# Modulation parts: transposes and a sum on VectorE in place of folding matmuls, in a two-layer trunk on one core

## What is computed

```
silu_c = jax.nn.silu(c)
mod = silu_c @ p["w_mod"][l] + p["b_mod"][l]
sh1, sc1, gt1, sh2, sc2, gt2 = jnp.split(mod[:, None, :], 6, axis=-1)
h = rmsnorm(x, p["norm1_g"][l]) * (1.0 + sc1) + sh1
...
x = x + gt1 * mix
h = rmsnorm(x, p["norm2_g"][l]) * (1.0 + sc2) + sh2
x = x + gt2 * hier_moe(h, p, l)
```

## Time and profile before

| | us |
|---|---|
| median of 3 runs | 1727.54 (1727.22 to 1728.41) |
| profiled execution, its own time | 1724.3 |
| its span, first to last instruction | 1722.7 |
| TensorE busy (matmuls) | 1675.0 |
| VectorE busy | 526.5 |
| ScalarE busy | 258.2 |
| GpSimd busy | 46.2 |

### The profile page before, as it was taken

One profiled execution on the slowest core, in us unless ns is written; L12 is line 12 of the kernel. 1 busy time (PEld: TensorE's weight loads), 2 busy tenths in 40 slices (PEclk: granted clock), 3 DMA queues, 4 the chain that ended last, 5 costly groups with the idle time before them and its releaser, 6 DMA issues. The chain is left out here.

```text
span 1722.7 us, 20395 instructions
## 1 busy us (share of the span) xinstructions
PE 1675.0 (97%) x8346; PEld 968.2 (56%) x8346; DVE 526.5 (31%) x1265; ACT 258.2 (15%) x502; POOL 46.2 (3%) x93
## 2 busy tenths in 40 slices
PE   6999999999999899999999999999999998999997
PEld 3677764445577554444447777554547765444443
DVE  1220210124611354333442212102263126233346
ACT  3110001101210231111131100010112013211111
POOL 0000000000100000000000000000010010000000
PEclk8999999999999989999999999999999999999999
DMA  9533556467943649999983336443887432899993
GB/s 400 235 138 125 217 201 256 179 245 296 406 188 135 244 148 388 421 421 421 423 345 132 127 120 256 184 147 148 327 347 301 147 134 112 329 422 421 421 421 162
DMA packets 47021, 451.69 MB, mean 262 GB/s; under 512 B 5632, under 2 KB 5888, under 8 KB 7504
## 3 DMA queue, kind: packets, MB, share of 16 engines
q1 hardware_dynamic: 43200, 409.65, 59.6%
q10 hardware_dynamic: 3456, 37.75, 5.2%
q0 software_dynamic: 272, 2.97, 0.4%
HBM read 411.16 MB, written 39.19 MB: 261 GB/s over the span
## 5 line engine op out<-in xcount | busy, mean ns | idle before, releaser
L657 PE MATMUL ps<-ring,work 128*64 128x512 f32 x1536 | 337.9, 595 | 2.9 <-ACT work L1055 2.6
L657 PE MATMUL ps<-ring,hT 128*32 128x128 f32 (+1 forms) x1920 | 319.9, 383 | 2.1 <-DMA ring<-stream 2.0
L657 PE MATMUL ps<-hT,ring 128*128 128x288 f32 x1280 | 314.4, 407 | 1.9 <-DVE work L1608 1.9
L657 PEld LDWEIGHTS ps<-hT,ring 128*128 128x128 f32 x1280 | 242.2, 190 | 71.6 <-issue 6.1
L657 PE MATMUL ps<-work,ring 128*128 128x288 f32 x1024 | 249.6, 406 | 4.1 <-issue 2.3
L657 PEld LDWEIGHTS ps<-ring,hT 128*32 128x32 f32 (+1 forms) x1920 | 154.8, 137 | 168.1 <-issue 163.0
L1055 ACT ACTIVATE work<-ps 128x512 f32<-128x512 f32 (+5 forms) x244 | 109.5, 467 | 837.4 <-PE ps L657 836.5
L657 PEld LDWEIGHTS ps<-ring,work 128*64 128x64 f32 x1536 | 111.7, 137 | 211.3 <-issue 211.0
L657 PEld LDWEIGHTS ps<-work,ring 128*128 128x128 f32 x1024 | 194.2, 190 | 58.7 <-issue 5.4
L657 PE MATMUL ps<-work 128*128 128x288 f32 (+6 forms) x800 | 189.5, 399 | 6.3 <-DVE hT L1751 2.6
L657 PEld LDWEIGHTS ps<-work 128*128 128x128 f32 (+2 forms) x800 | 125.1, 187 | 69.4 <-issue 36.4
(11 more groups left out here) (177 smaller groups left out, 846.8 us busy)
## 6 DMA issues: line engine op xcount, KB each, us to landing
ring<-stream SPq DMA_DIRECT2D x96, 2048.0 KB, 8.6
ring<-stream SPq DMA_DIRECT2D x192, 1024.0 KB, 10.2
state_sample_out<-ring ACTq DMA_DIRECT2D x16, 2048.0 KB, 10.0
state_out<-prm ACTq DMA_DIRECT2D x8, 512.0 KB, 11.4
prm<-params SPq DMA_DIRECT2D x1, 2608.5 KB, 25.8
prm<-params POOLq DMA_DIRECT2D x1, 2608.5 KB, 15.8
cst<-consts SPq DMA_DIRECT2D x1, 1649.0 KB, 19.2
xT<-x_in SPq DMA_DIRECT2D x1, 1152.0 KB, 5.4
```

Source lines behind the costliest of these rows:

```text
L657: return nc.tensor.matmul(out, lhsT, rhs, start=start, stop=stop, **k)
```

## The change

Each folding product with modfold becomes a plain transpose against the identity: fold_pending writes four 128x128 transposes into a tile modt of its own, one for each mod step. The four partial sums then lie side by side along the free axis (in each chunk of 128 columns, four blocks of 32, of which 9 columns are used). VectorE sums them with one tensor_reduce per mod step over a strided view, waits, and adds the bias (take_mod in place of take_mods). It does so at the next "mod" step of its own list or at the "fold" step, so VectorE now waits on TensorE 24 times for these tiles, where it was 6. The table of banks changes: modt tiles mostly take turns over banks 0 to 6; the last of "next" and of "gate" lie in bank 7, those of "last" in banks 3 and 4. Nothing moves among the loads, the products or ScalarE's copies.

```diff
+turn, waiting = 0, None
+def use_fold(b=None):
+    global turn, waiting
+    if waiting is not None:
+        use((*waiting, "modt"), turn % 7 if b is None else b)
+        turn += b is None
+    waiting = None
...
-        for _g in (g for g, group in GROUPS_OF_MODS.items() if _s == ("mod", group[0])):
-            use((_g, "modt"), YBANK)
         for _t in tiles_of(_s, _l):
             use((_l, _s, _t), turn % 7)
             turn += 1
+        if _s[0] == "mod" or _s[0] == "fold" and waiting is not None and FOLD_OF[waiting[1][1]][0:2] == (_l, _s[1]):
+            use_fold(YBANK if _s in (("fold", "next"), ("fold", "gate")) else None)
+        if _s[0] == "mod":
+            waiting = (_l, _s)
...
-            if LAST_MODS[_l]:
-                use(((_l, "last"), "modt"), 3)
+            for _n, _s in enumerate(LAST_MODS[_l]):
+                use((_l, _s, "modt"), 3 + _n)
...
                 l, step = pending.pop()
-                gl, name, n = FOLD_OF[step[1]]
-                key = ((gl, name), "modt")
-                wait_reads(pe, [(l, step, "modp")], free=key if n == 0 else None)
+                key = (l, step, "modt")
+                out = wait_free(pe, key, [(l, step, "modp")])
                 buf = modp[:, MOD_TURN[step[1]] % 2, :]
                 for c in range(4):
-                    at = (4 * n + c) * ROWS
-                    last = mm(ps[bank(key)][:, at:at + ROWS], buf[:, c * P:c * P + P], C("modfold"), True, True)
-                if n == len(GROUPS_OF_MODS[gl, name]) - 1:
-                    made(last, key)
+                    last = transposed(out[:, c * P:c * P + P], buf[:, c * P:c * P + P], C("ident"))
+                made(last, key)
...
-            def take_mods(group):
-
-                l, first = GROUPS_OF_MODS[group][0]
-                n = 4 * len(GROUPS_OF_MODS[group])
-                bias = (R("bmod") if l == 0 else bias_next)[:, 4 * first:4 * first + n].rearrange("p (f o) -> p f o", o=1).broadcast_to([P, n, ROWS])
-                out = wait_made(dve, (group, "modt"))
-                taken(dve.tensor_tensor(mod_of(l)[:, 4 * first:4 * first + n, :], cut(out[:, 0:n * ROWS], n, ROWS), bias, ALU.add), (group, "modt"))
+            waiting = []
+
+            def take_mod(group=None):
+
+                if not waiting or group is not None and FOLD_OF[waiting[0][1][1]][0:2] != group:
+                    return
+                key = (*waiting.pop(), "modt")
+                l, i = key[1][1]
+                bias = (R("bmod") if l == 0 else bias_next)[:, 4 * i:4 * i + 4].rearrange("p (f o) -> p f o", o=1).broadcast_to([P, 4, ROWS])
+                dst = mod_of(l)[:, 4 * i:4 * i + 4, :]
+                parts = wait_made(dve, key)[:, :].rearrange("p (c j r) -> p c r j", c=4, j=4)[:, :, 0:ROWS, :]
+                taken(dve.tensor_reduce(dst, parts, op=ALU.add, axis=AX.X), key)
+                settle()
+                dve.tensor_tensor(dst, dst, bias, ALU.add)
                 settle()
```

More of the change, by code:

```diff
@@ L133, in use @@
     used[b] += 1
-turn = 0
+turn, waiting = 0, None
[5 more added lines that the diff above has]
+    waiting = None
 for _l in range(DEPTH):
@@ L1544, in _ @@
                     kind, i = step
-                    if kind == "fold":
-                        if step == ("fold", "start"):
+                    if kind == "mod":
+                        if l == 0 and step == ("mod", (0, 0)):
                             dve.wait_ge(head_loaded, 48)
-                        take_mods((l, i))
+                        take_mod()
+                        waiting.append((l, step))
+                    elif kind == "fold":
+                        take_mod((l, i))
                     elif kind == "scale":
@@ L1565, in _ @@
                             if i == 1:
-                                take_mods((l - 1, "last"))
+                                for last in LAST_MODS[l - 1]:
+                                    waiting.append((l - 1, last))
+                                    take_mod()
                     elif kind == "affine":
```

## The result

| kernel | median us (range) | executions |
|---|---|---|
| before | 1727.97 (1727.22 to 1729.64) | 4 |
| after | 1711.07 (1708.35 to 1712.45) | 4 |

The profiled execution of after took 1712.45 us by its own time, 11.85 less than that of before (1724.3). So of the 16.9 us one pair of profiles shows about 70%, and the rest has to be found in the executions beside it.

The account below looks back on a forecast made before the run. TensorE, busy for 1675.0 of 1722.7 us, was taken to bound the kernel. Savings of 3.5 + 0.5 + 1.07 + 2.0 + 2.18 = 9.2 us off a 1727.5 us median gave 1718.3 us, range 1714.5 to 1723.5.

Parts of the forecast that it names:

- (a): Start, four folds: saves nothing, as TensorE then waits 1.96 us for the load of the first v weights.
- (b): Layer 0 among q, k and vr, eight folds: six alone save 2.94 us, the pair 0.57; together 3.5 us.
- (c): Layer 0 between o and experts, four folds: two before waits save nothing, third 0.5, fourth with bank effect 1.07 us.
- (f): Layer 1 between o and experts, two folds: first saves nothing, second 0.49 us; with the 1.69 bank wait gone, 2.18.
- The third fold: Layer 0 routing, at half clock: saves 0.87 us or only 0.49, by when the clock returns; 0.5 taken.
- (d): Last two folds of layer 0's experts, before layer 1: save nothing, as ScalarE's scaled tile sets the next start.
- (e): Layer 1 among q and k, four folds alone: save 4 x 0.49 = 2.0 us.
- B: Rival: the bank waits return elsewhere, another ScalarE copy or the packed tokens ending last; 1720.6 us, chance 0.09.
- C: Rival: transposes cost as much as the old pairs, only the 2.3 us bank effect is left; 1725.2 us, chance 0.05.
- A: Rival: clock stays low longer in layer 1 after 1424.6, plus a similar short slip; 1725.1 us, chance 0.10.
- D: Rival: slower, the clock staying low through all of layer 1's routing; 1740 us, chance 0.05.
- E: Rival: clock returns earlier in layer 0's gather, one short stretch of 3.4 us or more; 1716.6 or lower, chance 0.05.

Follow-up runs that it names:

- banks_only: The kernel before with its folding products kept and only the turn of the PSUM banks as in after; 1726.71 us, ratio 0.9989.
- the two halves: The change split: its bank turns alone on before (1726.71 us), and after with its transposes mostly in bank 7, other tiles keeping before's banks (1715.52 us).
- folds_wide: The kernel before with each folding matmul widened from 9 to 128 columns, the further results unused; 1718.55 us, ratio 0.9940.
- plain_identity: The kernel after with each transpose written as a plain fp32 matmul against the identity; 1716.27 us, ratio 0.9935.
- transposes_twice: The kernel after with each set of four transposes issued twice; 1714.45 us, ratio 0.9919.
- folds_twice: The kernel before with each fold's matmuls issued twice, still 9 columns wide; 1752.99 us, ratio 1.0142.
- the seven with 128 columns: The kernels with folds 128 columns wide: after, its repeat, four edits of it, and before with widened folds; medians 1711.07 to 1718.55 us.

## Why the prediction was right and wrong

**The price of a fold.** Nearly right: 0.43 us were forecast, 0.50 measured by the single row, a gain of 0.42 instead of 0.49. Over longer stretches a fold gained 0.50 (2.01 us over the four of layer 1).

**(a) Start.** The term was zero, on the ground that the wait ends with a DMA. The wait did not grow by what the folds lost, as was said: it was 1.96 us and is 1.73. In after it ends with ScalarE's scaled tile and no longer with the DMA; in before that tile, the first of eight in the row below, was there about half a microsecond ahead of 32.92, where the DMA's end lets TensorE start:

```profile
31.74 4.04 ACT L1055 ACTIVATE hT<-hT,mods,scaled 128x256 f32<-128x256 f32 x8 [2.00 <-DVE scaled L1321]
```

In banks_only, which has no sum, ScalarE ends the wait too, after 1.53 us. So 0.2 us of VectorE's sum lies on the path there, a small miss of the reading "VectorE is covered everywhere".

**(b) Layer 0, token folds.** 3.5 forecast; the shift goes from +0.94 to -2.58, so 3.52. The pair takes 312.57 - 311.20 = 1.37 us, of which 2 x 0.49 are transposes and 0.39 is the wait for ScalarE's copy that was foreseen, though it stands inside one row of eight.

**(c) and (f), routing.** The waits behind the first folds grow from 2.51 to 2.90 in both layers, as said. The wait for the choice stays at 1.73 instead of growing, since TensorE's work ahead of it took 0.34 us longer at a lowered clock (the choice comes 12.95 us after the logits' start, it was 12.99). The third fold was worth 1.73 - 0.49 = 1.24, more than either way I weighed, because the clock was back before it began and not during it. For the last one and the banks, read from g4 to the experts. In before g4 started at 616.64 and 1450.10 (timeline of before, both layers):

```profile
616.64 5.80 PE L657 MATMUL ps<-work 128*128 128x352 f32 x24
...
1450.10 5.80 PE L657 MATMUL ps<-work 128*128 128x352 f32 x24
```

To the experts it took 627.84 - 616.64 = 11.20 us and 1462.37 - 1450.10 = 12.27 us. In after it takes 620.44 - 610.30 = 10.14 and 1450.69 - 1440.55 = 10.14: 1.06 and 2.13 less, forecast 1.07 and 2.18. The packed tokens did not end last.

**(d) and (e).** 0 forecast, 0.01 measured. 2.0 forecast, 7.49 - 5.48 = 2.01 measured.

**The sum** of 9.2 us stands against 10.6 in span times clock (10.3 for the two halves); the rest of 1.4 us is little more than the scatter of that yardstick and is not placed. Rivals B and C are out by these rows.

**The step that failed is the clock.** I took its term as zero. It was worth 0.004 of the mean clock, about 7 us, which is all of the miss but about one. The argument for zero looked only at whether transposes hold the clock, by the retention's row. It did not ask what the 9-column matmuls they replace had been doing to it. The profile had a hint: the stretches at 0.50 from 598.6 and 1424.6 begin behind a fold and a wait, and I put them down to the wait alone. Nor did I look at all of the lost clock: the same trace has 3.4 us at 0.52 from 585.0 and 0.96 over the first 130 us (0.84 and 0.73 in the rows of the start), some 14 us beside the 17 us in the earlier trace rows; I never weighed that part. folds_wide shows that the fold's width is a cause too, with next to nothing else changed. Rivals A and D had the sign wrong, E the right one, but at one short stretch in one place, and with a chance of 0.05. In the profiled pair layer 0's gather gave back 3.4 us (13.6 us at 1.2 GHz became 6.8, twice E's stretch) and layer 1's logits 1.7; the start and the new stretch at 948.3 took 1.7 each, so that this pair shows less of the clock's gain than the medians do.

**The base** hid it. I added the 9.2 to the median by way of one profiled execution; that one had a clock of 0.990, at the top of what before shows in 35 executions (0.987 to 0.990). After's had 0.991, a little under its own mean of 0.992. So the two profiles differ by 11.85 us, the medians by 16.9. And a mean clock of 0.988 leaves 0.012 of 1727, some 20 us, that an edit can still win back; of that the prediction gave E a single stretch, 1.7 us. The range's low end, too, came out at 1714.8 by the terms that the prediction names for it (0.37, 0.41, 1.7 and 1.0 off 1718.3), not at 1714.5; that changes nothing, as 1711.07 lies below both.

**The rule on transposes.** folds_wide, plain_identity and transposes_twice spend 0.99, 1.00 and 0.93 us per fold on 128 columns, the last as transposes, and all three come to a clock of 0.994; before spends 0.92 us on 9 columns and comes to 0.988. The Trainium skill ("TensorE: Matmul & The Clock Gate", Part 4: PE-mode transpose) says that transposes don't count as busy in the same way. Here, for fp32 transposes of 128x128, the runs do not agree: issued for the same time, they held the mean clock as plain products did. After itself, with folds half as long, stays at 0.992; more of the same transposes raised it.

What stays open: which of the folds carry how much of the 0.004, since the low stretches wander between executions and each kernel has one profiled execution (13.6 us from 598.6 in before, and the like in banks_only and folds_twice, against at most 6.8 in the seven with 128 columns, is the largest difference that can be placed); why wide folds of half the length keep the clock in the routing but not at the start; and by which path doubling the sum costs clock.

## What to carry to other kernels

Price an edit on TensorE twice, by its length in the row and by the clock: here, replacing matmuls with few columns was worth 5 to 7 us through the clock and 7.5 through their time, and a useless widening (9 to 128 columns, 1 us more work) bought 10 us. Before a sum is set against one profiled execution, compare its granted clock with those of the other executions; 0.001 is 1.7 us of this kernel. When banks are renumbered, walk the table up to the tiles with fixed banks: that found 2.3 us of waits here, and banks_only then gained 2.3.

## What the runs showed of the hardware

- The granted clock answered to the width of the folds' matmuls: with the same count of instructions and nearly the same time, 0.988 at 9 columns and 0.994 at 128; with twice the count at 9 columns, 0.983. At 128 columns more time in them told as well: 0.992 with transposes of 0.50 us a fold, 0.994 with 0.93 us. In folds_twice TensorE, 19.07 of 20.6 us busy by its row, stood at 1.2 GHz throughout.
- An fp32 product of 9 columns takes nearly the row time of one with 128: four take 0.92 and 0.99 us (the median record is 257 and 275 ns); four transposes of 128 columns take 0.49 to 0.50.
- VectorE sums four blocks of 9 columns over a strided view of PSUM (144 to 36 elements) in 307 ns, and adds the bias in 196.
